# A hybrid trunk on one core: the second mixer's output projection in two parts, and the small triangular blocks ahead of the score blocks

## The chip, the core and the metric

The kernel runs on one core of a Trainium2 chip. The core has five engines with queues of their own, which meet only at semaphores: TensorE (PE in the profile, with its weight loads as PEld) multiplies, VectorE (DVE) and ScalarE (ACT) read and write both the core's memory and the banks into which TensorE writes, GpSimd (POOL) works on the core's memory alone, and SyncE (SP) issues the transfers. The metric is the device time of one execution in microseconds (us).

## What is computed

Two layers on 512 tokens of width 1024, each a mixer and an MLP with residuals, and a last norm. Everything is float32. The change is in layer 1:

```python
h = _rmsnorm(x, norm_mix[1])
p = h @ odd_w_in[0]                              # 1024 -> 2720
o_c = _rwkv7(p[..., :RWKV_IN], ...)              # 8 heads of 64: a recurrence over the tokens
o_d = _conformer_conv(p[..., RWKV_IN:], ...)     # gate, 31 taps in time, LayerNorm, swish: 512 channels
m = concatenate([o_c, o_d])                      # 512 + 512 channels
x = x + m @ odd_w_out[0]                         # 1024 -> 1024
f = square(relu(_rmsnorm(x, norm_ffn[1]) @ w_up[1]))
x = x + f @ w_down[1]
...
# inside _rwkv7, per head:
S = S * w_t + sa * (kk_t * a_t) + v_t * k_t ;  y_t = S r_t
```

## The kernel before

**Layout and precision.** Activations lie channels by tokens: tile k of `x` is 128 channels by 512 tokens. Each large product is made of three matmuls of rounded parts, high by high, low by high and high by low, 128x128 weights against 128x512, all summed in one bank (`cuts`, L994; `tile`, L999). A 128x1024 by 1024x512 product for one output tile is 24 such matmuls. Weights come in chunks of 1 MB, sixteen 128x128 blocks: SP loads chunk n into slot n % 2 once `lo_done` frees it, ScalarE rounds it to `w_hi` (`cut_hi`, or `cut` in four pieces), GpSimd then subtracts to `w_lo` in four pieces (L580) after `hi_done`, which comes with the last piece of the chunk. TensorE waits for `lo_done` before a chunk's first block. ScalarE may round chunk n only when chunk n-2's products are done (`gemm_done`).

**The second mixer** is ordered by hand: the lists `PE1`, `DVE1` and `ACT1` give each engine's steps one by one, and steps of different sort stand between each other. The steps:

- `slice t k`: three matmuls (channel tile k) of one of 22 tiles of the input projection, 176 in all; `ROWS` orders the tiles. Tiles 14 to 21 are the convolution's, in pairs (gate and value), 0 and 1 the low-rank parts, the rest k, v and r of four head pairs c = 0 to 3.
- For each head pair c: `zw`, `za`, `ks`, `kn`, `dyn` and `bonus` prepare; `scores c 0..3` multiply 128x256 blocks, which VectorE copies under a mask (`SC`, L1981, two copies a step); `scores c 4` makes the eight 8x8 diagonal blocks (L1352), VectorE picks them (L1990) and inverts them in six rounds of three small operations (`solve`, L2000 to L2004), `x_of` spreads the inverse. `tok_tr` transposes. `tx`, `dx`, `dxt` with level 3 to 6 double the inverse's block size four times, TensorE, ScalarE (`txc`) and VectorE (`xc`) by turns. Then the chain over the four token chunks n: `g` (L1452, L1456), ScalarE copies `G`, `u` (L1464), ScalarE copies `U`, `s` (L1472, L1474), VectorE updates the state `Sp` (L2058), `y` (L1488 to L1492), and `g` of the next n needs `Sp`. `post c 0..2` normalize and gate into `ym`.
- `tap c j`: the convolution on VectorE, 31 steps for each of four channel groups, each adding to the one before. After the last: `conv_mean`, `conv_sub`, squares, `conv_var`, `conv_root`, `conv_spread`, `conv_scale`, `conv_silu`.
- `m i` rounds channel tile i of the mixer's output for the output projection; `out t i` is one channel tile's three matmuls of output tile t. `M_TILES` puts tile 3, the last pair's, last.

Before, all eight channel tiles of an output tile are summed in one bank. `out` steps exist for output tiles 0 and 1 only; tiles 2 to 7 follow the mixer (`out_proj`). VectorE adds each finished tile to `x`, squares it, makes the low part of the normed input (`h_rest`) and adds up the squares (`residual`); ScalarE makes the high part (`h_cut`). `first_up` multiplies MLP tiles 0 and 1 channel tile by channel tile as `h_ready` allows, `stat` sums the squares over channels with 16 small matmuls, and `up(0, 1)` takes the MLP's second weight chunk.

## Time and profile before

| what | us |
|---|---|
| median of three timed runs | 1248.44 |
| lowest and highest | 1248.24 and 1249.92 |
| the profiled execution, device time | 1249.62 |
| its span, first to last instruction | 1247.8 |
| TensorE busy in the span | 1208.0 |
| VectorE busy in the span | 640.9 |
| second mixer with its output projection, first matmul to last | 546.6 to 885.4 |

A busy TensorE is not TensorE at its peak. Matmuls overlap, so a busy time says only that there was one in flight; what a matmul costs in a stream is the distance between two starts. The granted clock says at which of two levels, 2.4 and 1.2 GHz, TensorE ran: 1.00 is the upper.

### The profile page before, as it was taken

What the parts mean: (1) busy time and instruction counts of PE and PEld (TensorE: products, weight loads), DVE (VectorE), ACT (ScalarE), POOL (GpSimd) and SP (SyncE); (2) the same over time, 40 slices, a digit from 0 to 9 for tenths busy, and PEclk for the clock granted to TensorE, in tenths of its full rate; (3) what the DMA queues carried; (4) which work ended last, traced back from release to release, by engine and by line L of the source; (5) the groups of instructions that cost most, each with busy time, mean ns of one, the idle gap of its engine ahead of it and who ended that gap; (6) DMA issues with size and microseconds to landing.
All of it is one profiled execution on the core that took longest, in us unless ns stands there. A gap on an engine that the chain in (4) does not pass through costs nothing. (4 is left out here: it accounts for less than half of the span.)

```text
span 1247.8 us, 19837 instructions
## 1 busy us (share of the span) xinstructions
PE 1208.0 (97%) x7876; PEld 968.2 (78%) x7876; DVE 640.9 (51%) x1032; ACT 399.5 (32%) x578; POOL 501.3 (40%) x368
## 2 busy tenths in 40 slices
PE   7999999999999999999999998989999999999996
PEld 6877778888888888887777766757888888888885
DVE  4524655442114544446789889876545211444333
ACT  5634423222112222226353634343322211222110
POOL 0541435554445555545121220113545444555441
PEclk9999999999999999999999999879999999999998
DMA  7211222222322222231111110102222222222211
GB/s 278 102 68 68 74 96 68 101 101 102 101 101 82 89 98 101 101 101 68 35 69 35 36 68 2 35 2 74 96 102 101 101 101 83 86 101 101 101 67 68
DMA packets 17776, 104.97 MB, mean 84 GB/s; under 512 B 1968, under 2 KB 2480, under 8 KB 6064
## 3 DMA queue, kind: packets, MB, share of 16 engines
q1 hardware_dynamic: 17280, 103.67, 23.9%
q8 instruction: 49, 0.80, 0.3%
q10 hardware_dynamic: 432, 0.38, 0.1%
q14 instruction: 15, 0.12, 0.0%
HBM read 101.94 MB, written 2.10 MB: 83 GB/s over the span
## 5 line engine op out<-in xcount | busy, mean ns | idle before, releaser
L580 POOL TENSOR_TENSOR w_lo<-w_raw,w_hi 128x512 fp32r<-128x512 f32 x360 | 495.6, 1406 | 714.4 <-ACT w_hi L673 266.6
L1013 PE MATMUL ps<-h_hi,w_hi 128*128 128x512 f32 x688 | 275.9, 401 | 0.1
L1013 PE MATMUL ps<-h_lo,w_hi 128*128 128x512 f32 x688 | 268.4, 390 | 0.0
L1013 PE MATMUL ps<-h_hi,w_lo 128*128 128x512 f32 x688 | 268.3, 390 | 0.0
L673 ACT ACTIVATE w_hi<-w_raw 128x2048 fp32r<-128x2048 f32 x50 | 95.7, 1913 | 194.7 <-PE ps L1013 143.4
L1013 PEld LDWEIGHTS ps<-h_hi,w_hi 128*128 128x128 f32 x688 | 129.3, 188 | 35.5 <-issue 8.7
L1013 PEld LDWEIGHTS ps<-h_hi,w_lo 128*128 128x128 f32 x688 | 129.4, 188 | 27.6
L1013 PEld LDWEIGHTS ps<-h_lo,w_hi 128*128 128x128 f32 x688 | 129.5, 188 | 25.7 <-issue 1.0
L1013 PE MATMUL ps<-f_hi,w_hi 128*128 128x512 f32 x384 | 149.4, 389 | 0.0
L1013 PE MATMUL ps<-f_lo,w_hi 128*128 128x512 f32 x384 | 149.4, 389 | 0.0
L1013 PE MATMUL ps<-f_hi,w_lo 128*128 128x512 f32 x384 | 149.4, 389 | 0.0
L1630 DVE TENSOR_TENSOR f_hi<-relu 128x512 f32 x64 | 56.8, 888 | 154.7 <-ACT relu L648 152.8
L648 ACT ACTIVATE relu<-ps 128x512 f32<-128x512 f32 x56 | 33.5, 599 | 223.4 <-PE ps L1013 223.4
L2085 DVE SCALAR_TENSOR_TENSOR cv<-zpad,cols,cv 128x512 f32<-128x512 f32 x120 | 96.5, 804 | 2.3
L1648 DVE TENSOR_TENSOR scaled<-ps,rn 128x512 f32<-128x512 f32 x16 | 11.1, 692 | 146.7 <-PE ps L1013 112.1
L1013 PEld LDWEIGHTS ps<-f_hi,w_lo 128*128 128x128 f32 x384 | 72.1, 188 | 15.0
L1013 PEld LDWEIGHTS ps<-f_hi,w_hi 128*128 128x128 f32 x384 | 72.1, 188 | 15.0
L1013 PEld LDWEIGHTS ps<-f_lo,w_hi 128*128 128x128 f32 x384 | 72.1, 188 | 14.9
L1634 DVE TENSOR_TENSOR f_sq<-relu 128x512 f32<-128x512 f32 x64 | 72.1, 1127 | 0.0
L1658 DVE TENSOR_TENSOR scaled<-ps,rn 128x512 f32<-128x512 f32 x16 | 11.1, 692 | 102.1 <-PE ps L1013 74.9
L598 ACT ACTIVATE w_hi<-w_raw 128x2048 fp32r<-128x2048 f32 x20 | 38.2, 1910 | 58.6 <-PE ps L1013 41.8
L1637 DVE TENSOR_TENSOR f_lo<-f_sq,f_hi 128x512 f32 x64 | 46.0, 718 | 12.3 <-DVE f_sq L1634 12.3
(328 smaller groups left out, 1699.8 us busy)
## 6 DMA issues: line engine op xcount, KB each, us to landing
w_raw<-in_weights SPq DMA_DIRECT2D x91, 1024.0 KB, 4.8
x<-in_xT SPq DMA_DIRECT2D x8, 256.0 KB, 6.5
w_raw<-in_weights SPq DMA_DIRECT2D x8, 256.0 KB, 6.9
outT<-x SPq DMA_DIRECT2D x8, 256.0 KB, 2.0
...
```

What stands on the lines that cost most here:

```text
L580: piece = pool.tensor_tensor(w_lo[:, j, at], w_raw[:, j, at], w_hi[:, j, at].bitcast(f32), SUB)
L598: act.activation(w_hi[:, n % 2, :], w_raw[:, n % 2, :], ACT.Copy).then_inc(s("hi_done"), 1)
L648: act.activation(relu[:, g % 2, :], bank(g % 2), ACT.Relu).then_inc(s("relu_done"), 1)
L673: act.activation(w_hi[:, n % 2, :], w_raw[:, n % 2, :], ACT.Copy).then_inc(s("hi_done"), 1)
L1013: mm = pe.matmul(bank(gb(g) if isinstance(i, int) else g % 2), w, r, start=(k == 0 and m == 0), stop=(k == K - 1 and m == 2))
L1630: tt(f_hi[:, bass.ds(4 * i + c, 1), :].rearrange("p a n -> p (a n)"), relu[:, g % 2, :], relu[:, g % 2, :], MUL).then_inc(s("fhi_done"), 1)
L1634: tt(f_sq[:, :], relu[:, g % 2, :], relu[:, g % 2, :], MUL).then_inc(s("fsq_done"), 1)
L1637: tt(f_lo[:, bass.ds(4 * i + c, 1), :].rearrange("p a n -> p (a n)"), f_sq[:, :], F(f_hi[:, bass.ds(4 * i + c, 1), :].rearrange("p a n -> ...
L1648: tt(scaled[:, j, :], bank((gd + j) % 2), rn[:, :], MUL)\
L1658: tt(scaled[:, d % 2, :], bank(g % 2), rn[:, :], MUL).then_inc(s(f"gemm_evac{g % 2}"), 1)
L2085: stt(cv[:, c, :], zpad[:, c % 2, j:j + SEQ], col("conv_w", TAPS * c + j), cv[:, c, :], MUL, ADD)\
```

## The change

The output projection's channel tiles are split into seven early ones (pairs 0 to 2 and the convolution) and the late one of the last pair, tile 3. The early parts of all eight output tiles are `out` steps in `PE1`, most of them between the steps of the last pair's chain; VectorE adds them to `x` (`add t`). The late part is 24 matmuls after the mixer (`late`), with a second addition to `x` (`late_adds`). The squares for the norm move to ScalarE (`late_cuts`) and their channel sums to TensorE, 16 small matmuls for each channel tile between the parts of `first_up` (`late_sums`). The weights' chunks are packed in the new order, with 3, 2, 2 and 1 finished tiles to the four chunks. `scores c 4` becomes `corner c` and goes ahead of the four `scores` steps, into banks 4 and 6. The taps of two channel groups have semaphores of their own and take turns. The convolution's projection tiles come earlier in `ROWS`, and all three lists are new. Semaphores of the set-up are merged.

```diff
+EARLY_M, LAST_M = [0, 1, 2, 4, 5, 6, 7], 3
+KE = len(EARLY_M)
+OUT1 = [3, 2, 2, 1]
-ROWS = [0, 2, 4, 3, 14, 15, 5, 7, 6, 1, 16, 17, 8, 10, 9, 18, 19, 11, 13, 12, 20, 21]
+ROWS = [0, 2, 14, 15, 4, 3, 5, 7, 16, 17, 6, 1, 8, 10, 18, 19, 9, 20, 21, 11, 13, 12]
...
+        def tap_done(c, n):
+
+            return s(f"tap_done{c % 2}"), TAPS * (c // 2) + n
...
+            ("out", 6, 0), ("out", 6, 1), ("y", 3, 3), ("out", 6, 2), ("out", 6, 3), ("post", 3, 0),
...
+            def late_cuts():
+
+                for k in range(KD):
+                    h_cut(3, k)
+                    if k >= 2:
+                        act.wait_ge(s("late_sums"), k - 1)
+                    act.activation((xsq, ssq)[k % 2][:, :], x[:, k, :], ACT.Square).then_inc(s("late_sq"), 1)
+                    for part in {5: (0,), 6: (1, 2), 7: (3,)}.get(k, ()):
+                        if part == 0:
+                            act.wait_ge(s("late_mm"), KD)
+                        cut(N_MLP1 + 1, part)
+                load_sqrt(3)
...
+            def late(t):
+
+                at = KE * KD + t
+                n, blk = N_OUT1 + at // 16, at % 16
+                if t == 0:
+                    pe.wait_ge(s("lo_done"), n + 1)
+                    pe.wait_ge(s("m_lo_done"), 2 * KD)
+                if t == 3:
+                    for last in (6, 7):
+                        pe.wait_ge(*evacuated(FIRST_TILE[N_OUT1] + last))
+                if t >= 5:
+                    pe.wait_ge(s("late_add"), t - 4)
+                for m, (w, r) in enumerate(cuts(n % 2, blk, LAST_M, M_HI1[LAST_M], M_LO1[LAST_M])):
+                    mm = pe.matmul(bank(late_bank(t)), w, r, start=(m == 0), stop=(m == 2))
+                mm.then_inc(s("late_mm"), 1)
+
+            def late_sums(k):
+
+                pe.wait_ge(s("late_sq"), k + 1)
+                for t in range(TT):
+                    for q in range(0, P, 32):
+                        mm = pe.matmul(ps[q:q + 32, 7, t:t + 1], (xsq, ssq)[k % 2][:, t * P + q:t * P + q + 32], ONES[:, 0:1],
+                                       start=(k == 0 and t == 0), stop=(k == KD - 1 and t == TT - 1))
+                mm.then_inc(s("late_sums" if k < KD - 1 else "stat_done"), 1)
...
-                        pe.wait_ge(s("lo_done"), nu + 1)
+                        if layer == 0:
+                            pe.wait_ge(s("lo_done"), nu + 1)
+                        else:
+                            late(0)
+                            late(1)
                         for k in range(KD):
+                            if layer and k + 2 < KD:
+                                late(k + 2)
+                            if layer and k == 0:
+                                pe.wait_ge(s("lo_done"), nu + 1)
                             pe.wait_ge(*wait_k(k))
...
+                            if layer:
+                                late_sums(k)
...
-            out_proj(N_OUT1 + 1, N_MLP1, M_HI1, M_LO1)
             mlp(1)
...
+            def late_adds():
+
+                for t in range(KD):
+                    dve.wait_ge(s("late_mm"), t + 1)
+                    tt(x[:, t, :], x[:, t, :], bank(late_bank(t)), ADD).then_inc(s("late_add"), 1)
+                    h_rest(3, t)
...
+            def add(t):
+
+                g = FIRST_TILE[N_OUT1] + t
+                dve.wait_ge(s("gemm_done"), g + 1)
+                tt(x[:, t, :], x[:, t, :], bank(g % 2), ADD).then_inc(s(f"gemm_evac{g % 2}"), 1)
...
-            residual(N_OUT1, 3)
+            late_adds()
             mlp(1)
```

What TensorE has in a row at three places. First, in the last pair's chain, from its second `g` (state and scores) over `u`, `s` and `y` to its third, before:

```order
L1452 MATMUL ps<-Sp,AR 64x64 x4
L1456 MATMUL ps<-vtok,SC 64x64 x4
L1490 MATMUL ps<-SC,U 64x128 x2
L1492 MATMUL ps<-SC,vtok 64x128 x2
L1464 MATMUL ps<-G,XT 64x64 x4
L1472 MATMUL ps<-U,btok 64x64 x2
L1474 MATMUL ps<-vtok,ktok 64x64 x2
L1488 MATMUL ps<-AR,Sp 64x128 x2
L1490 MATMUL ps<-SC,U 64x128 x2
L1492 MATMUL ps<-SC,vtok 64x128 x2
L1452 MATMUL ps<-Sp,AR 64x64 x4
```

and now, from the same `g` up to its `u` and a part of what follows:

```order
L1526 MATMUL ps<-Sp,AR 64x64 x4
L1530 MATMUL ps<-vtok,SC 64x64 x4
L1629 MATMUL ps<-m_hi,w_hi 128x512
L1629 MATMUL ps<-m_lo,w_hi 128x512
L1629 MATMUL ps<-m_hi,w_lo 128x512
L1629 MATMUL ps<-m_hi,w_hi 128x512
L1629 MATMUL ps<-m_lo,w_hi 128x512
L1629 MATMUL ps<-m_hi,w_lo 128x512
L1538 MATMUL ps<-G,XT 64x64 x4
L1629 MATMUL ps<-m_hi,w_hi 128x512
```

The parts of the output projection have moved in between the chain's steps.

Second, around the last `y` (L1488 to L1492) of the third pair's chain, with the last pair's first `scores` ahead of it, before:

```order
L1340 MATMUL ps<-AR,kT 128x256 x2
L1488 MATMUL ps<-AR,Sp 64x128 x2
L1490 MATMUL ps<-SC,U 64x128 x2
L1492 MATMUL ps<-SC,vtok 64x128 x2
L1013 MATMUL ps<-h_hi,w_hi 128x512
L1013 MATMUL ps<-h_lo,w_hi 128x512
L1013 MATMUL ps<-h_hi,w_lo 128x512
L1013 MATMUL ps<-h_hi,w_hi 128x512
L1013 MATMUL ps<-h_lo,w_hi 128x512
L1013 MATMUL ps<-h_hi,w_lo 128x512
L1340 MATMUL ps<-AR,bT 128x256 x2
```

and now (L1414 is `corner`, L1427 `scores`, L1449 and L1451 `tok_tr`):

```order
L1414 MATMUL ps<-AR,bT 32x32 x32
L1538 MATMUL ps<-G,XT 64x64 x4
L1562 MATMUL ps<-AR,Sp 64x128 x2
L1564 MATMUL ps<-SC,U 64x128 x2
L1566 MATMUL ps<-SC,vtok 64x128 x2
L1427 MATMUL ps<-AR,bT 128x256 x2
L1427 MATMUL ps<-AR,kT 128x256 x2
L1427 MATMUL ps<-AR,bT 128x256 x2
L1427 MATMUL ps<-AR,kT 128x256 x2
L1427 MATMUL ps<-AR,bT 128x256 x2
L1427 MATMUL ps<-AR,kT 128x256 x2
L1449 MATMUL ps<-cen,vT 128x128 x4
```

The projection's slices that stood here have moved ahead of the third pair's chain.

Third, in the MLP's first two tiles, where before the 48 matmuls stood in one row, now for each channel tile:

```order
L1108 MATMUL ps<-m_hi,w_hi 128x512
L1108 MATMUL ps<-m_lo,w_hi 128x512
L1108 MATMUL ps<-m_hi,w_lo 128x512
L1151 MATMUL ps<-h_hi,w_hi 128x512
L1151 MATMUL ps<-h_lo,w_hi 128x512
L1151 MATMUL ps<-h_hi,w_lo 128x512
L1151 MATMUL ps<-h_hi,w_hi 128x512
L1151 MATMUL ps<-h_lo,w_hi 128x512
L1151 MATMUL ps<-h_hi,w_lo 128x512
L1116 MATMUL ps<-mats,ssq 32x1 x16
```

The late part (L1108) and the sums of squares (L1116) have moved in between.

## Rows read from the trace of the kernel before

**Rows 1.** Busy time by stretch; columns as in its first row (PEclk: granted clock).
```profile
core 0: us, PE busy (x) PEld busy (x) DVE busy (x) ACT busy (x) POOL busy (x), PEclk, DMA share, GB/s
766.25:797.75 31.50, 27.04 (x338) 18.32 (x337) 26.01 (x66) 12.35 (x25) 5.44 (x4) 1.00 0.10 35
797.75:818.10 20.35, 18.78 (x282) 14.62 (x282) 19.02 (x33) 5.22 (x14) 0.00 (x0) 0.75 0.01 2
804.00:814.00 10.00, 9.96 (x139) 8.39 (x136) 9.45 (x17) 0.93 (x3) 0.00 (x0) 0.50 0.01 2
821.00:831.30 10.30, 8.99 (x91) 6.28 (x86) 8.30 (x14) 2.14 (x6) 0.00 (x0) 0.50 0.00 0
546.60:886.30 339.70, 320.50 (x3420) 239.33 (x3418) 271.35 (x522) 146.99 (x300) 82.52 (x60) 0.96 0.14 48
```

**Rows 2.** TensorE in order of time: start, us, line, idle before.
```profile
766.25 0.45 PE L1456 MATMUL ps<-vtok,SC 128*64 128x64 f32 x8
797.75 1.12 PE L1398 MATMUL ps<-xc,SC 64*64 64x32 f32 x32
818.10 0.45 PE L1456 MATMUL ps<-vtok,SC 128*64 128x64 f32 x8 [0.41 <-ACT XT L913]
885.36 0.39 PE L1076 MATMUL ps<-h_hi,w_hi 128*128 128x512 f32 x1
896.18 0.39 PE L1076 MATMUL ps<-h_lo,w_hi 128*128 128x512 f32 x1
896.41 0.39 PE L1076 MATMUL ps<-h_hi,w_lo 128*128 128x512 f32 x1
896.73 0.43 PE L1037 MATMUL ps<-mats,ssq 128*32 128x1 f32 x32
897.09 0.50 PE L1013 MATMUL ps<-h_hi,w_hi 128*128 128x512 f32 x1
```

**Rows 3.** TensorE's waits from 560 to 900 us: total, times, longest.
```profile
PE ps L1452 <- DVE Sp L2058: 4.1, 8, 0.6
PE ps L1340 <- DVE SC L1981: 3.5, 4, 1.4
PE ps L1464 <- ACT G L926: 3.4, 9, 0.4
```

**Rows 4.** VectorE in order of time: a lone tap, last pair's scores and inversion, chained taps.
```profile
757.52 0.70 DVE L2085 SCALAR_TENSOR_TENSOR cv<-zpad,cols,cv 128x512 f32<-128x512 f32 x1
758.13 0.29 DVE L2023 COPY_PREDICATED xc<-masks,ps 128x128 f32<-128x128 uint8 x1
...
788.74 1.35 DVE L1981 COPY_PREDICATED SC<-masks,ps 128x512 f32<-128x512 uint8 x2
789.99 1.00 DVE L1990 COPY_PREDICATED lt<-masks,ps 128x64 f32<-128x64 uint8 x4
791.82 0.22 DVE L2000 STREAM_SHUFFLE r<-z 128x64 f32<-128x64 f32 x1
792.60 0.22 DVE L2000 STREAM_SHUFFLE r<-z 128x64 f32<-128x64 f32 x1
796.99 0.71 DVE L2016 STREAM_TRANSPOSE xc<-xtc 128x512 f32<-128x512 f32 x1
814.83 5.47 DVE L2085 SCALAR_TENSOR_TENSOR cv<-zpad,cols,cv 128x512 f32<-128x512 f32 x7
```

**Rows 5.** VectorE, ScalarE and GpSimd at the residual, and one rounding piece (L812).
```profile
885.56 0.69 DVE L1612 TENSOR_TENSOR x<-x,ps 128x512 f32<-128x512 f32 x1 [0.90 <-PE ps L1013]
887.04 0.75 DVE L1593 SCALAR_TENSOR_TENSOR h_lo<-x,cols,h_hi 128x512 fp32r<-128x512 f32 x1
886.29 0.72 ACT L624 ACTIVATE h_hi<-x,cols 128x512 fp32r<-128x512 f32 x1 [4.71 <-DVE x L1612]
836.28 0.62 ACT L812 ACTIVATE w_hi<-w_raw 128x512 fp32r<-128x512 f32 x1
888.89 5.03 POOL L580 TENSOR_TENSOR w_lo<-w_raw,w_hi 128x512 fp32r<-128x512 f32 x4 [5.39 <-ACT w_hi L598]
```

More of the change, by code:

```diff
@@ L428, in build @@
-            ("scores", 3, 4), ("slice", 21, 2), ("conv_mean", 0), *run("tok_tr", 3, 0, 3), ("post", 2, 0),
-            *run("slice", 21, 3, 8), ("tx", 3, 3, 0), ("tx", 3, 3, 1), ("post", 2, 1), ("dx", 3, 3, 0),
[5 rows of a table removed]
-            ("u", 3, 3), ("y", 3, 3), *run("conv_var", 0, 4), ("out", 0, 2), ("conv_spread",), ("post", 3, 0),
-            ("post", 3, 1), *run("out", 1, 0, 3), ("post", 3, 2), ("out", 0, 3), ("out", 1, 3), ("out", 0, 4),
-            ("out", 1, 4), ("out", 0, 5), ("out", 1, 5), ("out", 0, 6), ("out", 1, 6), ("out", 0, 7), ("out", 1, 7),
+            ("slice", 0, 3), ("slice", 2, 3), ("stat",), ("slice", 0, 4), ("slice", 2, 4), ("slice", 0, 5),
@@ new lines, in build @@
+            ("dx", 2, 4, 1), ("slice", 12, 0), ("slice", 12, 1), ("post", 1, 2), ("slice", 12, 2), ("slice", 12, 3),
[4 rows of a table added]
+            ("g", 2, 3), ("corner", 3), ("u", 2, 3), ("y", 2, 3), *run("scores", 3, 0, 3), ("tok_tr", 3, 0),
+            ("scores", 3, 3), ("tok_tr", 3, 1), ("tok_tr", 3, 2), ("post", 2, 0), ("conv_mean", 0),
+            ("conv_mean", 1), ("tx", 3, 3, 0), ("tx", 3, 3, 1), ("dx", 3, 3, 0), ("dx", 3, 3, 1), ("conv_mean", 2),
+            ("conv_mean", 3), ("tx", 3, 4, 0), ("tx", 3, 4, 1), ("dx", 3, 4, 0), ("dx", 3, 4, 1), ("post", 2, 1),
@@ L438, in build @@
+            *run("out", 7, 2, 7),
         ]
         DVE1 = [
[L441 to L444 removed]
@@ new lines, in build @@
+            ("zero", 4), ("evac_a", 2), ("zero", 5), ("zero", 6), ("evac_b", 2), ("evac_a", 14), ("evac_b", 14),
+            ("evac_a", 15), ("ks_v", 0), ("scan", 0), ("kn_v", 0), ("dyn", 0, "at"), ("evac_a", 4),
+            ("dyn", 0, "ab"), *run("tap", 0, 0, 4), ("evac_a", 3), ("dyn", 0, "bt"), ("evac_b", 4), ("evac_b", 3),
+            ("dyn", 0, "k2"), ("dyn", 0, "kt"), ("dyn", 0, "rt"), ("dyn", 0, "rk"), ("evac_a", 5), ("bonus", 0),
+            ("tap", 0, 4), ("corner", 0), ("solve", 0, 6), ("evac_b", 5), ("solve", 0, 5), ("solve", 0, 4),
@@ new lines, in build @@
+            ("solve", 0, 3), ("scores", 0, 0), ("dec", 0), ("evac_a", 7), ("scores", 0, 1), ("tap", 0, 5),
+            ("scores", 0, 2), ("evac_a", 16), *run("tap", 0, 6, 9), ("solve", 0, 2), ("scores", 0, 3),
+            ("tap", 0, 9), ("evac_b", 7), ("evac_b", 16), ("scan", 1), ("solve", 0, 1), ("x_of", 0), ("evac_a", 17),
+            ("tap", 1, 0), ("tap", 0, 10), ("tap", 1, 1), ("tap", 1, 2), ("tap", 0, 11), *run("tap", 1, 3, 9),
+            ("dx", 0, 3, 0), ("ks_v", 1), ("tap", 1, 9), ("tap", 0, 12), ("evac_a", 6), ("dx", 0, 3, 1),
@@ new lines, in build @@
+            ("evac_b", 18), ("tap", 1, 25), ("evac_a", 19), ("dxt", 1, 5), ("tap", 2, 0), ("tap", 2, 1),
+            ("post_v", 0, 2), ("tap", 2, 2), ("dyn", 2, "rk"), *run("tap", 2, 3, 7), ("tap", 1, 26), ("tap", 2, 7),
+            ("evac_a", 9), ("post_v", 0, 3), ("s", 1, 0), ("evac_b", 9), ("bonus", 2), ("tap", 1, 27),
+            ("corner", 2), ("s", 1, 1), ("tap", 2, 8), ("tap", 1, 28), ("tap", 2, 9), ("solve", 2, 6),
+            ("tap", 2, 10), ("tap", 1, 29), *run("tap", 2, 11, 14), ("tap", 1, 30), ("tap", 2, 14), ("s", 1, 2),
@@ new lines, in build @@
+            ("tap", 2, 15), ("tap", 2, 16), ("evac_a", 20), ("solve", 2, 5), ("solve", 2, 4), ("solve", 2, 3),
+            ("solve", 2, 2), ("tap", 2, 17), ("solve", 2, 1), ("evac_b", 20), ("scores", 2, 0), ("evac_a", 21),
+            ("tap", 3, 0), ("scores", 2, 1), ("tap", 3, 1), ("evac_a", 11), ("scores", 2, 2), ("evac_b", 11),
+            ("tap", 3, 2), ("x_of", 2), ("tap", 3, 3), ("scores", 2, 3), ("tap", 3, 4), ("tap", 2, 18),
+            *run("tap", 3, 5, 8), ("scan", 3), ("tap", 3, 8), ("post_v", 1, 0), ("tap", 3, 9), ("tap", 3, 10),
@@ L2149, in rest @@
         return r
-    out += rest(i["even_w_out"][0], i["w_up"][0], i["w_down"][0])
+    out += rest([_both(i["even_w_out"][0], R(256 * n), R(256 * n + 128)) for n in range(4)], i["w_up"][0], i["w_down"][0])
     xw, xg = list(range(1536, 1600)), list(range(1600, 1696))
```

361 lines of the change are left out of this document (178 added, 183 removed), and 38 rows, old and new, of tables (ACT1, PE1).

## The prediction

> **What bounds the kernel now.** I looked first at busy time by stretch, then at TensorE's order of time, then at who waits for whom, then at VectorE's order, always inside the second mixer, since the change leaves the rest as it is. The row for the whole mixer and projection [rows 1] gives TensorE 320.5 of 339.7 us busy and VectorE 271.4. So TensorE is the bound on average, with 19.2 us of true idle, and VectorE, at 80%, has little room. The idle time is in handoffs of a chain: above all the state update and the copy of `G` [rows 3], 0.4 to 0.6 us each. Beside it, two stretches of 10 us have a granted clock of 0.50, the lower of the two levels (1.2 GHz), right where the last pair's inversion and chain leave TensorE's matmuls small and scattered [rows 1]. They cost up to 5 us each. That and the last chain's waits is what the change can win at the end; the question is what it gives for it.
>
> I cut the time from the first matmul of the mixer (546.6) to the first of the MLP's second weight chunk (897.09) into five stages at marks that both versions have [rows 2]: third pair's chain begins (766.25), last pair's first `tx` (797.75), last pair's chain begins (818.10), `first_up` begins (885.36), `up(0, 1)` begins (897.09).
>
> **Unit costs.** A matmul of 128x512 takes 0.23 us from start to start (896.18 to 896.41) [rows 2], so a slice or an `out` part takes 0.69. A switch to a small group costs 0.09 more (0.32 from 896.41 to 896.73), and I take 0.2 for going and coming back. Sixteen sums take 0.36. On VectorE a lone tap takes 0.61 until the next instruction starts (757.52 to 758.13); in a row where each waits for the one before, seven take 5.47, so 0.79 [rows 4]. A `scores` pair is 1.25, the diagonal pick 1.0, a `solve` round 0.78, `x_of` 1.5 [rows 4].
>
> **Stage 1, to the third pair's chain.** The lists, counted, put 176 slices here instead of 165: 11 x 0.69 = 7.6 us of TensorE work that comes earlier and is not new. Other work up to the mark is equal. Against it stand waits that the new order can avoid: most of the 3.5 us for `SC` [rows 3], since other steps now stand between the score blocks. But the first pair's chain loses half of its cover of slices, which at 0.4 to 0.55 a handoff gives back some 1.4. VectorE has 4 fewer us of chained taps in the whole mixer (28 chained ones against 66 in the lists, 0.12 each), and enough lead here: by counts it reaches each handoff some 18 to 25 us of own work earlier than TensorE does, and starts some 19 later. So TensorE still sets the pace. 7.6 - 3.0 = 4.6: **+4.6**.
>
> One rule of the Trainium skill speaks about the taps. VectorE: DVE Perf Modes, section The DRAIN you can't avoid, has it that a next instruction waits for the pipe to empty, chained or not. Then alternating two groups would save nothing. By that rule the sum would be up to 4 us longer where VectorE is the bound; the trace has 0.61 alone and 0.79 in a chain, so it disagrees, and the measurement is used.
>
> **Stage 2, to the last pair's first `tx`.** Before: 31.5 us with TensorE 27.0 busy and VectorE 26.0 [rows 1]. The 11 slices are gone from here, so TensorE has about 27.0 - 7.6 + 2.1 (two sums of the convolution) = 21.5. VectorE has more: 12 taps instead of 8, six steps of `dyn`, three copies out, the state updates, four score pairs (5.0), the pick (1.0), six rounds (4.7), `x_of` (1.5); with 12 x 0.68 for the taps, between the lone and the chained one, I get 28.7. `tx` needs the inverse, so VectorE decides. Its head waits for `g`, `u`, `s` (2.5), and 1 us for score blocks. **32 us, +0.5**, and TensorE stands still for 8 to 10 of them. The corner blocks that lead don't shorten this: VectorE is full from end to end.
>
> **Stage 3, to the last chain.** Before 20.35, 10 of it at the low clock. Without the one `out` part and its wait that is 19.3; at full clock maybe 15.5. Now `conv_var`, `conv_spread` and three parts replace two `conv_mean`: +3.2, and VectorE has the convolution's end and the last taps between the turns: I come to 19.5 for the turns. Then 13 more `out` parts stand ahead of `g`: 9.0. The clock: this stretch and the one before are as scattered as the ones that fell to 0.50 before, so I add 3; for VectorE beside a weight chunk on GpSimd I allow 1.5, which no row prices alone. **33.0 us, +12.7**, of which 16 parts (11.0) are work brought forward.
>
> **Stage 4, to the end of the early projection.** Before 67.26. Now 40 parts x 0.69 = 27.6, the chain's own matmuls and `post` 10.8, 14 switches x 0.2 = 2.8: **41.2 us, -26.1**. No wait is left: between a `g` and its `u` stand two parts, 1.4 us, against 0.4 for the copy; `Sp` is covered by one or two. The weight chunks come in time: a chunk needs four roundings (0.62 each, 0.5 start to start) and GpSimd's 5.0 [rows 5], about 8 to 10 with what ScalarE does between, while TensorE has 11 to 12 us before it needs the block. That cover is thin: 2 us.
>
> **Stage 5, to `up(0, 1)`.** Before 11.73. Now 24 late matmuls (5.5), 48 (10.9), eight sums (8 x 0.36 = 2.9) and some 16 half switches (1.8): 21.1. Waits on top: the first `h_ready` needs the addition (0.69), the high part (0.72), the low part (0.75) [rows 5], 2.3 us after `late(0)`, with 1.4 of cover: 0.9. The last such one adds 0.4. Then the new one: the chunk for `up(0, 1)` may be rounded only after all eight late tiles (`late_mm`), and its pieces stand between two `h_cut`s and two squares. From the end of `late(7)`: 4 pieces (2.1), two `h_cut`s (1.4), two squares (1.1), about 4.7; GpSimd 5.0 and latencies: done at 10. TensorE has for that only the last three channel tiles, 3 x (1.4 + 0.36 + 0.2) = 6. It stands 4 us. 21.1 + 0.9 + 0.4 + 3.8 = **26.2 us, +14.5**. Before, its lower part was done at 888.89 + 5.03 = 893.9 [rows 5], 3 us ahead of the 897.09 of `up(0, 1)`.
>
> **Sum.** 4.6 + 0.5 + 12.7 - 26.1 + 14.5 = +6.2. The profiled execution took 1249.62, so 1255.8; the median of the runs is 1.2 lower: **1254.6 us**.
>
> **Bounds of what no row shows.** The clock in stages 2 and 3: from none low (-3) to 20 us of it on the path (+7). Stage 1: from all waits gone and no loss (-2.5) to VectorE late at the third pair (+4). The chunk wait: 0, if the roundings slip in earlier, to 5. Stage 2: 29.7 (VectorE's work with 1 us of waits) to 35.
>
> **The rivals.** *Faster, the cover works.* VectorE is not the bound in stage 2: it arrives with its taps and scores done, because it worked through the waits of stage 1. Then stage 2 is TensorE's 21.5 and handoffs, 25; with no gap the clock stays at the upper level, 3 less in stage 3. 1254.6 - 7 - 3 = 1244.6, and 1241 with the early waits gone too. For it: VectorE has 68 us free in the mixer [rows 1]. Against: its instructions in stage 2 depend on that stage's own blocks, apart from 12 taps; only without six of them and with `solve` unbroken does it come under 27. It decides if VectorE's busy share in stage 2 is under 85%.
>
> *Nothing moves.* The gain of stage 4 and its price cancel, with the clock term at 0 and half of the chunk wait: 1254.6 - 3 - 2 = 1249.6.
>
> *Slower by more, the clock.* The low level comes with thin activity: before, it came twice around the last pair. Now TensorE has 21.5 of 32 us to do there and then a chain of turns. If some 20 us run at 0.50 with the turns on the path, that is +7 to 1262. The Trainium skill says it too, in TensorE: Matmul & The Clock Gate, What's actually happening: activity releases the throttle and its lack brings it back. By that the emptied stage 2 would lower the clock; the dense rows of stage 4, which replace the second low stretch, speak for the upper level there.
>
> **How the numbers follow.** About 0.2%, 2.5 us, is what a measurement can tell from no change. The forecast (1251 to 1258) 0.50, the clock rival (1258 to 1266) 0.14, nothing moves (1246 to 1251) 0.16, faster 0.20. So slower 0.64, same 0.16, faster 0.20. For 8 in 10 the range goes from 1242 to 1264.
>
> **What would show it.** Right: VectorE over 90% busy between the third pair's chain and the last pair's `tx`, with TensorE's longest waits there on `xc`; no wait of `u` and `s` in the last chain; a wait on `w_lo` of some 4 us at the MLP's second chunk. Wrong: a granted clock of 1.00 throughout and stage 2 under 28 us, or no wait on `w_lo`; then it is faster.

## The result, and the profile after

| | us |
|---|---|
| changed kernel, median of 14 runs | 1257.02 (1253.67 to 1261.63) |
| kernel before, 14 runs beside them | 1249.94 (1244.78 to 1253.86) |
| ratio, with its 95% interval | 1.0067 (1.0052 to 1.0082) |
| profiled execution of the changed kernel, device time and span | 1259.28 and 1256.3 |

The change costs 0.67%, 8.4 us. It was forecast at +6.2, 1254.6 us. The stages have the same marks as in the prediction. First the busy times of the changed kernel by stretch; the columns are those of [rows 1]. The rows are the five stages, then all of them, then what stands behind them.

```profile
547.73:772.93 225.20, 220.24 (x2299) 163.81 (x2297) 188.45 (x381) 106.86 (x223) 54.55 (x40) 0.99 0.15 51
772.93:805.94 33.01, 24.83 (x307) 15.96 (x306) 27.30 (x69) 8.36 (x19) 0.00 (x0) 0.79 0.01 1
805.94:833.91 27.97, 27.82 (x464) 21.71 (x463) 18.36 (x35) 18.90 (x36) 10.14 (x8) 1.00 0.12 40
833.91:874.78 40.87, 40.83 (x327) 29.36 (x327) 9.08 (x16) 11.85 (x25) 14.94 (x13) 1.00 0.23 78
874.78:901.98 27.20, 21.53 (x329) 15.57 (x329) 15.68 (x23) 15.13 (x24) 6.92 (x6) 0.97 0.12 40
547.73:901.98 354.25, 335.25 (x3722) 246.41 (x3720) 258.87 (x520) 161.09 (x327) 86.55 (x65) 0.97 0.14 48
901.98:1256.30 354.32, 344.06 (x1568) 284.56 (x1568) 126.58 (x151) 72.62 (x61) 165.33 (x120) 0.98 0.27 92
```

The kernel before has for the same stretches as a whole, up to its mark 897.09 and from there on:

```profile
546.61:897.09 350.48, 331.27 (x3497) 248.05 (x3495) 273.38 (x524) 151.84 (x305) 87.55 (x64) 0.97 0.15 50
897.09:1247.80 350.71, 340.46 (x1578) 281.85 (x1568) 129.48 (x155) 74.80 (x63) 165.48 (x120) 0.99 0.26 91
```

| stage | before | after | difference | forecast |
|---|---|---|---|---|
| 1, to the third pair's chain | 219.64 | 225.20 | +5.6 | +4.6 |
| 2, to the last pair's first `tx` | 31.50 | 33.01 | +1.5 | +0.5 |
| 3, to the last pair's chain | 20.35 | 27.97 | +7.6 | +12.7 |
| 4, to the end of the early projection | 67.26 | 40.87 | -26.4 | -26.1 |
| 5, to `up(0, 1)` | 11.73 | 27.20 | +15.5 | +14.5 |
| sum of the five | 350.48 | 354.25 | +3.8 | +6.2 |
| behind `up(0, 1)`'s start | 350.71 | 354.32 | +3.6 | 0 |
| ahead of the mixer | 546.61 | 547.73 | +1.1 | 0 |

So the mixer is only 3.8 us longer, and nearly as much again is lost behind it. The 1.1 us ahead of the mixer have no part in the change: over the kernels profiled here that start lies between 545.9 and 548.4.

TensorE's true idle in the five stages is 354.25 - 335.25 = 19.0 us, against 19.2 before. The parts hid the last chain's waits, and others opened. The longest of TensorE's waits in stage 2, and then those in stage 5, of the changed kernel (line that waited, what ended the wait, total us, times, longest):

```profile
PE ps L1427 <- DVE SC L2063: 3.8, 3, 2.1
PE ps L1538 <- ACT G L968: 1.5, 3, 0.8
```

```profile
PE ps L1055 <- POOL w_lo L609: 4.2, 1, 4.2
PE ps L1151 <- issue: 1.0, 1, 1.0
PE ps L1151 <- DVE h_lo L1668: 0.5, 2, 0.4
```

The lower clock moved likewise. These are the stretches of 8 us of the changed kernel in which the granted clock was under 0.99, up to 912 us:

```profile
688.00:696.00 8.00, 7.34 (x132) 6.21 (x131) 5.48 (x12) 3.72 (x8) 5.41 (x4) 0.98 0.10 16
696.00:704.00 8.00, 8.00 (x64) 6.40 (x62) 6.66 (x13) 0.82 (x2) 0.00 (x0) 0.81 0.30 119
...
776.00:784.00 8.00, 5.49 (x68) 3.76 (x66) 6.92 (x13) 2.83 (x7) 0.00 (x0) 0.60 0.00 0
784.00:792.00 8.00, 7.55 (x122) 4.33 (x122) 5.23 (x16) 1.07 (x3) 0.00 (x0) 0.76 0.01 4
792.00:800.00 8.00, 4.19 (x26) 2.99 (x24) 7.67 (x24) 0.17 (x1) 0.00 (x0) 0.88 0.00 0
800.00:808.00 8.00, 7.34 (x116) 5.12 (x116) 7.79 (x18) 4.15 (x9) 0.00 (x0) 0.91 0.01 2
...
896.00:904.00 8.00, 3.85 (x43) 2.83 (x43) 5.74 (x6) 3.08 (x4) 7.93 (x6) 0.78 0.12 16
904.00:912.00 8.00, 8.00 (x30) 6.41 (x29) 4.32 (x5) 0.60 (x1) 4.68 (x3) 0.79 0.53 195
```

With two levels, a mean of 0.81 over 8 us is (1 - 0.81) x 2 x 8 = 3.0 us at the lower one. Added up, the eight rows hold 23.8 us. The same sum for the kernel before, over 720 to 736 and 800 to 832, gives 23.8 too. They lie elsewhere: 13.6 in the third pair's chain and the score blocks behind it, where the slices had been taken out, and 6.8 at the wait for the chunk, from 900.5 to 907.3. The second and third stretch of before, around the last pair, are gone. Neither sum holds the end of the kernel, where the last 11.1 us of the changed kernel are at the lower level and the last 7.0 of the kernel before.

The wait and what follows it, TensorE in order of time (start, us, line, and in brackets the idle time ahead and what ended it):

```profile
901.98 0.80 PE L1055 MATMUL ps<-h_hi,w_hi 128*128 128x512 f32 x1 [4.15 <-POOL w_lo L609]
902.57 0.63 PE L1055 MATMUL ps<-h_lo,w_hi 128*128 128x512 f32 x1
903.00 0.63 PE L1055 MATMUL ps<-h_hi,w_lo 128*128 128x512 f32 x1
```

TensorE stands still for 4.15 us, and then a matmul takes 0.43 from start to start, where it takes 0.23 at the upper level [rows 2]. The clock had come down inside the wait, where it costs nothing; 5.3 of the 6.8 us lie behind the wait, and they cost 2.5: from `up(0, 1)` to the MLP's last large matmul the changed kernel needs 340.4 us and the kernel before 337.9. The other 1.1 of the +3.6 behind the mark lie in the last norm, most of it in eight matmuls that run at the upper level in the kernel before (first row) and at the lower one in the changed kernel:

```profile
1238.87 1.16 PE L1057 MATMUL ps<-mats,rrms 128*128 128x128 f32 x8 [0.60 <-DVE rrms L1578]
1246.43 2.08 PE L1124 MATMUL ps<-mats,rrms 128*128 128x128 f32 x8 [0.59 <-DVE rrms L1653]
```

This end varies from one execution to the next: the lower level has the last 7 to 8 us in seven of the thirteen executions profiled here and the last 10 to 11 in five, with and without a wait for the chunk ahead of it (e11 and the changed kernel; e9 and e1).

### The profile page after: what moved, and what is told of

The parts are those of the page before. It is cut to its first block, busy times and chain, and to the rows that moved or that the text cites. A ratio compares the mean times of both kernels' runs of the same rounds, so it can differ in the third digit from the quotient of the medians.

```text
span 1256.3 us, 20279 instructions
## 1 busy us (share of the span) xinstructions
PE 1216.0 (97%) x8100; PEld 969.6 (77%) x8100; DVE 623.5 (50%) x1023; ACT 406.6 (32%) x599; POOL 500.2 (40%) x368
## 4 chain that ended last, share of the span: by engine, by line
PE 91%; DVE 3%; ACT 2%; POOL 2%; issue 2%; DMA 0%; DVEq 0%; SPq 0%; POOLq 0%; ACTq 0%
PE ps L1055 60%; PE ps L1185 7%; PE ps L1242 4%; PE ps L1629 3%; PE ps L1219 2%; POOL w_lo L609 2%; PE ps L1151 1%; PE ps L1427 1%; PE ps L1472 1%; PE ps L1495 1%; PE ps L1354 1%; PE ps L1108 1%; PE ps L1538 1%; PE ps L1530 0%; PE ps L1124 0%
## 5 line engine op out<-in xcount | busy, mean ns | idle before, releaser
L702 ACT ACTIVATE w_hi<-w_raw 128x2048 fp32r<-128x2048 f32 x50 | 95.6, 1913 | 194.7 <-PE ps L1055 143.4
L1055 PEld LDWEIGHTS ps<-h_hi,w_lo 128*128 128x128 f32 x688 | 130.2, 189 | 27.9
L1055 PE MATMUL ps<-f_hi,w_hi 128*128 128x512 f32 x384 | 149.4, 389 | 0.0
L2167 DVE SCALAR_TENSOR_TENSOR cv<-zpad,cols,cv 128x512 f32<-128x512 f32 x120 | 90.7, 776 | 1.0
L1730 DVE TENSOR_TENSOR scaled<-ps,rn 128x512 f32<-128x512 f32 x16 | 11.1, 692 | 146.7 <-PE ps L1055 112.1
L1740 DVE TENSOR_TENSOR scaled<-ps,rn 128x512 f32<-128x512 f32 x16 | 11.1, 692 | 102.1 <-PE ps L1055 74.9
L1185 PE MATMUL ps<-f_hi,w_hi 128*128 128x512 f32 x128 | 49.8, 389 | 0.0
```

Of the source, the lines that this page charges most:

```text
L702: act.activation(w_hi[:, n % 2, :], w_raw[:, n % 2, :], ACT.Copy).then_inc(s("hi_done"), 1)
L1055: mm = pe.matmul(bank(gb(g) if isinstance(i, int) else g % 2), w, r, start=(k == 0 and m == 0), stop=(k == K - 1 and m == 2))
L1185: mm = pe.matmul(bank((gd + j) % 2), w, r, start=(k == 0 and m_ == 0), stop=(k == HALF_K - 1 and m_ == 2))
L2167: stt(cv[:, c, :], zpad[:, c % 2, j:j + SEQ], col("conv_w", TAPS * c + j), cv[:, c, :], MUL, ADD)\
```

## Experiments

Times are medians, ratios go against runs of the kernel before on the same chip. The stages are those of one execution each, and how much of it ran at the lower level differs between executions of the same steps: the 1.6 us by which e1 and e6 are shorter in stage 1 are such a stretch, at 696. e9's profiled execution is the fastest of its twelve runs. The stages of all profiled executions, in us; the first two rows are those above:

| kernel | 1 | 2 | 3 | 4 | 5 | behind | median | ratio (95%) |
|---|---|---|---|---|---|---|---|---|
| before | 219.6 | 31.5 | 20.4 | 67.3 | 11.7 | 350.7 | 1249.9 | |
| changed | 225.2 | 33.0 | 28.0 | 40.9 | 27.2 | 354.3 | 1257.0 | 1.0067 (1.0052 to 1.0082) |
| e1, roundings earlier | 223.6 | 33.0 | 27.8 | 40.9 | 23.0 | 351.8 | 1249.9 | 1.0005 (0.9989 to 1.0021) |
| e2, wait filled | 225.2 | 33.2 | 27.8 | 40.9 | 27.3 | 350.9 | 1252.6 | 1.0028 (1.0013 to 1.0042) |
| e3, stage 2 filled | 225.1 | 29.7 | 35.9 | 40.9 | 27.2 | 352.3 | 1258.6 | 1.0065 (1.0045 to 1.0084) |
| e4, six taps cut | 225.2 | 31.5 | 35.1 | 40.9 | 27.2 | 352.3 | 1256.8 | 1.0061 (1.0036 to 1.0086) |
| e5, chain bare | 225.2 | 33.0 | 21.9 | 59.2 | 27.8 | 352.2 | 1269.1 | 1.0150 (1.0121 to 1.0178) |
| e6, sums on VectorE | 223.6 | 32.1 | 27.9 | 40.9 | 25.5 | 351.7 | 1252.2 | 1.0011 (0.9994 to 1.0028) |
| e7, corner last | 228.3 | 42.3 | 27.8 | 40.9 | 27.2 | 352.1 | 1267.5 | 1.0139 (1.0109 to 1.0169) |
| e8, e1 and more filled | 225.1 | 29.7 | 30.9 | 40.9 | 23.0 | 351.6 | 1250.4 | 1.0002 (0.9986 to 1.0019) |
| e9, sums in the wait | 225.2 | 29.8 | 27.8 | 40.9 | 22.8 | 350.7 | 1249.6 | 1.0006 (0.9986 to 1.0027) |
| e10, e9 and a little filled | 225.2 | 29.7 | 29.1 | 40.9 | 22.8 | 354.3 | 1249.5 | 1.0009 (0.9987 to 1.0030) |
| e11, e9 with a later low part | 227.5 | 32.8 | 27.8 | 40.9 | 24.6 | 352.9 | 1254.6 (one run; the kernel before beside it 1255.0) | |

### e1: the four roundings earlier

```diff
-                    for part in {5: (0,), 6: (1, 2), 7: (3,)}.get(k, ()):
-                        if part == 0:
-                            act.wait_ge(s("late_mm"), KD)
+                    for part in {1: (0,), 2: (1,), 5: (2,), 6: (3,)}.get(k, ()):
+                        if part >= 2:
+                            act.wait_ge(s("late_mm"), 4 * (part - 1))
```

> The four roundings of the chunk for up(0, 1) stand at channel tiles 1, 2, 5 and 6 instead of 5, 6, 6 and 7; the first two overwrite blocks of output tile 7's early part, the third waits for four late tiles, the fourth for all eight. Theory: the changed kernel loses 4.15 us to the wait for this chunk and, because TensorE stood still, runs some 6 us at the lower clock behind it (0.43 instead of 0.23 from start to start, about 3 us). With the last piece some 3.5 us sooner, GpSimd's 5 us end at about 898.3, so of the wait under 1 us is left and the clock stays up: 1257.0 - 3.7 - 3 = 1250 us, ratio to before 1.001. Rival: the wait only moves to the next chunk or to the sums and the low clock has another cause: under 2 us gained, 1255 or more.

Measured: 1249.9 us. The wait is 0.6, and no lower clock stands behind it. The four pieces of the low part start at 889.90. That is 17.5 us after the stage's start, and in the changed kernel it was 21.3 (896.07), so they come 3.8 us earlier in the stage.

```profile
889.90 5.46 POOL L609 TENSOR_TENSOR w_lo<-w_raw,w_hi 128x512 fp32r<-128x512 f32 x4 [16.45 <-ACT w_hi L854]
895.42 0.50 PE L1055 MATMUL ps<-h_hi,w_hi 128*128 128x512 f32 x1 [0.61 <-POOL w_lo L609]
```

Stage 5 loses 4.2 us and what lies behind it 2.5, together 6.7; the medians are 7.1 apart. (Stage 1 is 1.6 shorter because this execution lacked the stretch at the lower clock at 696.) So where the four roundings stand and what they wait for is worth nearly the whole loss. In the changed kernel ScalarE stood for 2.9 us, waiting for the eighth late tile ahead of its first piece, which needs none of them, and then had all four pieces, two high parts and two squares to do before GpSimd could start; in e1 only the last piece is left behind that tile. The edit changed place and threshold at once, and no run parts the two.

### e2: the wait filled

```diff
                     def up(i, j, wait_k=None):
+                        if layer and half == 0 and isinstance(i, int):
+                            pe.wait_ge(s("late_add"), KD)
+                            for _ in range(16):
+                                pe.matmul(bank(2), H_HI[0][:, 0:P], H_HI[0], start=True, stop=True)
                         pe.wait_ge(s("lo_done"), 2 * i + (nu + j + 1))
```

> 16 added matmuls of 128x512 into a bank that nobody needs stand ahead of the wait for the chunk of up(0, 1); the results are unused. Their 3.7 us lie inside the wait of 4.15. Theory: the low clock behind the wait is due to TensorE standing still, so it stays at the upper level and about 3 us come back with the wait's end unchanged: 1254 us, ratio 1.004. Rival: the low clock comes from elsewhere, or the added work delays the chunk: 1257 us, ratio 1.0067.

Measured: 1252.6. Stage 5 is as long as in the changed kernel, the chunk comes no sooner, and yet 3.4 us come back behind it, 2.5 of them right behind the wait and 0.9 in the kernel's last norm, which the edit doesn't touch:

```profile
896.56 3.92 PE L1162 MATMUL ps<-h_hi 128*128 128x512 f32 x16
900.87 0.50 PE L1055 MATMUL ps<-h_hi,w_hi 128*128 128x512 f32 x1 [0.39 <-POOL w_lo L609]
901.21 0.40 PE L1055 MATMUL ps<-h_lo,w_hi 128*128 128x512 f32 x1
901.45 0.39 PE L1055 MATMUL ps<-h_hi,w_lo 128*128 128x512 f32 x1
```

The starts are 0.23 apart at once, against 0.43 above. A wait of 4.15 us on this path cost 4.2 + 2.5 in the changed kernel's profile, and the second part is the clock alone. It isn't always as much: e3, e4, e5 and e7 have the same wait of 4.15 to 4.18 with 3.4 us at the lower level where the changed kernel has 6.8, and there it costs 1.5. The Trainium skill says in TensorE: Matmul & The Clock Gate, section What's actually happening, that activity releases the throttle and its lack brings it back; the pair of runs agrees.

### e3 and e8: large matmuls in the waits of stages 2 and 3

In e3, with evacuated banks and no use of the results (`warm n` is n matmuls of 128x512):

```diff
+            ("warm", 2), ("u", 2, 1), ("warm", 1), ("s", 2, 1), ("y", 2, 1), ("warm", 2), ("g", 2, 2), ("warm", 1),
+            ("u", 2, 2), ("warm", 1), ("s", 2, 2), ("y", 2, 2), ("bonus", 3), ("g", 2, 3), ("corner", 3), ("u", 2, 3),
+            ("warm", 1), ("y", 2, 3), ("scores", 3, 0), ("warm", 6), ("scores", 3, 1), ("warm", 8), ("scores", 3, 2),
```

> 25 added matmuls of 128x512 with unused results stand in TensorE's waits between the third pair's second u and the last pair's third score blocks, one or two at a handoff, six and eight between score blocks. Theory: stage 2 (33.0 us) loses about 2 to 3 us to the lower clock in the third pair's chain, where slices no longer fill the gaps; with the gaps filled the clock is 1.00 there and the stage takes about 31, total 1254.5. It doesn't get shorter than 29.5, since VectorE has 27.3 us of work in it. Rival A: VectorE sets the whole stage and the clock there costs nothing: 33.0, total 1257. Rival B: the added matmuls delay the handoffs more than the clock gives back: 34, total 1258.

Measured: 1258.6. Stage 2 did what the theory says, 29.7 at a clock of 1.00. But stage 3 grew by 8, which neither side had:

```profile
771.77:801.46 29.69, 26.23 (x330) 16.66 (x329) 27.34 (x69) 8.35 (x19) 0.00 (x0) 1.00 0.01 2
801.46:812.50 11.04, 10.24 (x295) 7.72 (x294) 9.03 (x17) 6.66 (x15) 5.00 (x4) 1.00 0.01 3
812.50:830.00 17.50, 17.43 (x145) 14.36 (x142) 8.77 (x17) 12.34 (x22) 1.21 (x2) 0.51 0.18 62
```

For 17 us, from the end of the convolution's sums (matmuls of one column) and a turn of the inversion on, TensorE is busy nearly without a gap, at half speed. e8 has e1's edit, the same fills, and three more matmuls at each of four places among those turns:

```diff
-("dx", 3, 4, 1), ("post", 2, 1), *run("conv_var", 0, 3), ("post", 2, 2), ("conv_var", 3), ("tx", 3, 5, 0), ("conv_spread",),
+("dx", 3, 4, 1), ("warm", 3), ("post", 2, 1), ("warm", 3), *run("conv_var", 0, 3), ("post", 2, 2), ("warm", 3), ("conv_var", 3),
+("tx", 3, 5, 0), ("conv_spread",), ("warm", 3),
```

> The earlier roundings and the matmuls in the last waits of the third chain, and 12 more of 128x512 (unused results) between the turns of the last pair's inversion, where filling the third chain's waits alone was followed by 17 us at the lower clock from the convolution's small sums on and stage 3 grew from 28.0 to 35.9. Theory: the clock falls behind stretches in which TensorE has only small matmuls; large ones between them keep it up: stage 2 is 29.7, stage 3 about 28 + 2.8, total 1249.9 - 3.3 + 2.8 = 1249.4. Rival: the lower clock comes sooner or later whatever stands there, one stretch of 10 to 17 us around the last pair; then it falls within stages 3 or 4 again and the total is 1255 or more.

```profile
772.44:802.13 29.69, 26.22 (x330) 16.65 (x329) 27.34 (x69) 8.35 (x19) 0.00 (x0) 1.00 0.01 2
802.13:833.01 30.88, 30.74 (x476) 23.59 (x475) 18.89 (x35) 18.90 (x36) 10.18 (x8) 1.00 0.10 36
```

Measured: 1250.4, as the theory has it. 12 matmuls (2.8 us) took away a stretch that had cost 8. That isn't the profiled execution alone: the mean clock is 0.992 to 0.996 in all twelve runs of e8, 0.989 to 0.993 in the twelve of e1, and 0.987 to 0.990 in the six of e3, which also has the wait for the chunk. But 29.69 + 30.88 is 60.6, and e1 without any of it has 60.8: what the clock gives back, the added work takes. So in these runs the clock follows what TensorE does, and unused work buys nothing. Why the changed kernel and e1 run stage 3 at 1.00, with the same steps there as e3, no run settles. It can fall there without added matmuls too: in e4 below it did, for 17 us of this stage.

### e4: six taps cut

```diff
+            SHORT = {(2, 26), (3, 25), (2, 27), (3, 26), (3, 27), (2, 28)}
...
+                    w = 8 if (c, j) in SHORT else SEQ
```

Six of the convolution's taps work on 8 of the 512 columns, so this kernel leaves out a part of the convolution.

> Work is left out: six of the convolution's taps that stand ahead of the last pair's inverse on VectorE handle 8 columns instead of 512, so the convolution's part of the output isn't the reference's. Theory: VectorE sets the end of stage 2, so 6 x about 0.5 us come off it: 33.0 becomes 30.0, total 1254. Rival: the handoffs of score blocks and the clock set it; the taps lie in waits and stage 2 stays at 32.5 to 33, total 1257.

Measured: 1256.8, between the two: stage 2 falls by 1.5, half of the 3.0, and all of it behind the third pair's last state update, which comes 12.95 us into the stage in both kernels. VectorE, which in the changed kernel had no wait from the pick of the corner blocks to the inverse, now waits for score blocks, 0.65 and 0.31 us at two of the four (the idle time stands in brackets):

```profile
792.87 1.33 DVE L2063 COPY_PREDICATED SC<-masks,ps 128x512 f32<-128x512 uint8 x2 [0.65 <-PE ps L1427]
```

So VectorE is the bound of the second half of stage 2, but the score blocks' round trips lie only a microsecond or so behind it. The profiled execution, at 1262.3 the slowest of its five, also had 17 us at the lower clock in stage 3, as e3 had.

### e5: the chain bare

The order of the last pair's chain and of the parts, each line a list of steps (the additions to `x` and the roundings, in VectorE's and ScalarE's lists, move along and aren't shown):

```diff
+            ("g", 3, 0), ("u", 3, 0), ("s", 3, 0), ("y", 3, 0), ("g", 3, 1), ("u", 3, 1), ("s", 3, 1), ("y", 3, 1),
+            ("g", 3, 2), ("u", 3, 2), ("s", 3, 2), ("y", 3, 2), ("g", 3, 3), ("u", 3, 3), ("y", 3, 3), *run("out", 0, 3, 7),
+            ("post", 3, 0), *run("out", 1, 0, 7), ("post", 3, 1), *run("out", 2, 0, 7), ("post", 3, 2), *run("out", 3, 0, 7),
...
```

> Undoes the cover: the last pair's chain runs bare, and all early parts from the fourth of output tile 0 on stand behind its last y, with the additions to x and the roundings of their weights moved behind the chain too. Theory: the parts inside the chain save its handoffs; bare, the chain has about 12 waits of 0.4 to 0.6 us (6 us) and runs at the lower clock for a part (3 us), and gives back 12 switches (2.4): last chain plus projection 7 us longer than 28.0 + 40.9, total 1264. Rival: the parts cost the chain as much as they hide, since the chain's own steps are few: within 2 us, 1257. In both cases stage 5 stays at 27.

Measured: 1269.1, 12 us slower than the changed kernel (10 by the ratios to the kernel before). Stages 3 and 4 together take 81.1 instead of 68.8. The bare chain, by stretch and by TensorE's two longest waits in it:

```profile
826.60:850.00 23.40, 18.81 (x189) 13.27 (x192) 1.36 (x5) 5.55 (x13) 4.94 (x4) 0.56 0.14 46
```

```profile
PE ps L1525 <- ACT XT L950: 3.5, 1, 3.5
PE ps L1533 <- ACT G L963: 2.0, 4, 0.8
```

With those for `U` and `Sp` the waits are 8 us, of which the 3.5 for the finished inverse (`XT`) had not been in the expectation, and a clock of 0.56 over 23.4 us is 20.6 us at the lower level. In the changed kernel TensorE was busy for 40.83 of 40.87 us there, at 1.00. Of the 12.2 us, the waits make 8, so that some 4 are left for the clock, an estimate, since the switches that fall away and the moved roundings weren't measured by themselves. The cover works, and that is part of its worth.

### e6, e9 and e11: who adds up the squares

e6 takes e1 and has VectorE add ScalarE's squares, with one sum over channels at the end:

```diff
+                        if t > 1:
+                            dve.wait_ge(s("late_sums"), t - 1)
+                        tt(ssq[:, :], ssq[:, :], (xsq[:, :], scaled[:, 0, :])[t % 2], ADD).then_inc(s("late_sums"), 1)
...
-                            if layer:
-                                late_sums(k)
```

> On top of the earlier roundings (1249.9): VectorE adds up the squares that ScalarE makes, and TensorE sums them once, with 16 small matmuls instead of 8 x 16 amid first_up. Theory: TensorE's seven sums less (0.36 each) and seven switches less (0.15 each) come off a stretch in which TensorE is the bound: stage 5 from 23.0 to 19.4, if the chunk's low part is there in time; it comes with the eighth late tile, which is 6 x 0.5 = 3 us sooner as well, so most is kept: 1246.9, ratio 0.998. VectorE has 2.1 us a channel tile against TensorE's 2.1. Rival: the addition delays the low part h_lo and TensorE waits for it: 1250, ratio 1.0005.

Measured: 1252.2, and stage 5 is 25.5, longer than e1's 23.0. The rival held: TensorE waits 4.6 us for `h_lo`, six times, because the addition stood behind the low part. e9 puts it into the 0.79 that VectorE waits for ScalarE:

```diff
                     tt(x[:, t, :], x[:, t, :], bank(late_bank(t)), ADD).then_inc(s("late_add"), 1)
+                    if t > 1:
+                        late_square(t - 1)
                     h_rest(3, t)
```

> The same as with the sums of squares on VectorE, but each addition stands between x's addition and the low part, where VectorE waits 0.79 us for ScalarE's high part, and not behind the low part. Theory: behind the low part it made a period of 2.74 us a channel tile (0.68 + 0.79 + 0.75 + 0.68 less overlaps) against TensorE's 2.1 to 2.3, and TensorE waited 4.6 us on h_lo; inside the wait the period is about 2.15, so the waits on h_lo go and stage 5 falls from 25.5 to about 20 to 21, total 1249.9 - 2.5 = 1247.4, ratio 0.998. Rival: ScalarE's high part and square, or the chunk's low part for up(0, 1), set the pace: stage 5 stays at 23, total 1250.

Measured: 1249.6, and stage 5 is 22.8, hardly shorter than e1's 23.0, though TensorE waits for `h_lo` only twice, 0.5 and 2.2 us, at the last two channel tiles. The loss is in the last one. VectorE and GpSimd of e9:

```profile
884.72 0.69 DVE L1698 TENSOR_TENSOR ssq<-ssq,scaled 128x512 f32<-128x512 f32 x1
885.60 0.75 DVE L1669 SCALAR_TENSOR_TENSOR h_lo<-x,cols,h_hi 128x512 fp32r<-128x512 f32 x1 [0.19 <-ACT h_hi L653]
...
886.86 1.66 DVE L1698 TENSOR_TENSOR ssq<-ssq,xsq 128x512 f32<-128x512 f32 x1
888.44 1.74 DVE L1669 SCALAR_TENSOR_TENSOR h_lo<-x,cols,h_hi 128x512 fp32r<-128x512 f32 x1
886.68 6.33 POOL L609 TENSOR_TENSOR w_lo<-w_raw,w_hi 128x512 fp32r<-128x512 f32 x4 [15.39 <-ACT w_hi L855]
```

As soon as GpSimd makes the chunk's low part, the same two operations take 1.66 and 1.74 instead of 0.69 and 0.75. e11 tests that, with the fourth rounding behind the eighth square (`7: (3,)` instead of `6: (3,)`):

> The kernel with the sums in VectorE's wait, its chunk's fourth rounding one channel tile later (behind the eighth square), so that GpSimd starts its low part some 2 us later, behind VectorE's last h_lo. Theory: VectorE's last three operations on the core's own memory took 1.66, 1.74 and 1.77 us, where the ones before took 0.69 and 0.75, because GpSimd worked at the same time; now the sum of the seventh square and the last low part take 0.69 and 0.75 again, TensorE's wait of 2.17 us for h_lo falls under 0.6, and the wait for the chunk's low part grows by 1 to 1.5 instead, with stage 5 at 23 to 24. Rival: those durations belong to the operations or to ScalarE's cuts beside them; they stay at 1.7 and stage 5 grows by the whole 2 us.

```profile
891.86 0.68 DVE L1698 TENSOR_TENSOR ssq<-ssq,xsq 128x512 f32<-128x512 f32 x1
892.74 0.75 DVE L1669 SCALAR_TENSOR_TENSOR h_lo<-x,cols,h_hi 128x512 fp32r<-128x512 f32 x1 [0.19 <-ACT h_hi L653]
893.82 7.67 POOL L609 TENSOR_TENSOR w_lo<-w_raw,w_hi 128x512 fp32r<-128x512 f32 x5 [17.53 <-ACT w_hi L855]
899.87 0.79 PE L1056 MATMUL ps<-h_hi,w_hi 128*128 128x512 f32 x1 [4.30 <-POOL w_lo L609]
```

The durations fall back to 0.68 and 0.75, and TensorE's longest wait for `h_lo` to 0.5. In their place stands a wait of 4.30 for the chunk, where it had been 0.7 and 1 to 1.5 more were expected. Stage 5 is 24.6, longer than the 23 to 24 expected: the durations go the way of the theory, and the stage grows by 1.8, nearly what the rival said. The lower level comes inside the wait and lasts 6.8 us, 4.6 of them behind it, much as in the changed kernel. It is one run of its kernel; the row's durations, not its time, are the evidence.

### e7: the corner blocks last again

For the last pair alone (TensorE's list is shown; VectorE's and the semaphore waits follow it):

```diff
-("g", 2, 3), ("corner", 3), ("u", 2, 3), ("y", 2, 3), *run("scores", 3, 0, 3), ("tok_tr", 3, 0), ("scores", 3, 3), ...
+("g", 2, 3), ("u", 2, 3), ("y", 2, 3), *run("scores", 3, 0, 4), ("corner", 3), ("tok_tr", 3, 0), ...
```

> Undoes one part for the last pair alone: its 8x8 corner blocks come behind its four score blocks again, and VectorE picks and inverts them after its copies of the scores, with the same taps in between. Theory: VectorE is full from the third pair's last state update on (27.3 us of work in 33.0), so the order of its work moves the inverse by no more than its waits, 1 us: stage 2 is 33 to 34, total 1257 to 1258. Rival: the lead of the corner is what hides the scores' round trips; without it VectorE waits for each of the four score blocks and the six rounds stand alone behind them: 36 us, total 1260.

Measured: 1267.5, 9 to 10 us slower than the changed kernel; even the rival was too mild. Stage 2 is 9.2 longer. (The 3 us in stage 1 are lower clock that the edit has no part in.) VectorE's longest waits in that stage:

```profile
DVE SC L2070 <- PE ps L1434: 5.6, 4, 2.0
DVE Sp L2147 <- PE ps L1573: 2.7, 2, 1.7
```

A score block's round trip (TensorE's multiplication, VectorE's copy, then the next) takes 2.6 us at the upper clock, of which VectorE works 1.3 and a tap 0.7; the rounds of the inversion had filled the rest. Now they stand behind the four trips, and TensorE, busy for 29.1 of 42.3 us, runs 20.5 us at the lower clock from 797 on, beside the 10.2 in the third pair's chain. How the 9 us divide between the exposed trips and that clock no run shows.

### e10: e9 with a little filled

The fills of e3, and one matmul where e8 has three.

> The same, with the 25 added matmuls in the third chain's and the scores' waits, and four instead of twelve between the last turns. Theory: a few large matmuls keep the clock up at a third of the price: stage 2 29.7, stage 3 29, total 1247.4 - 3.3 + 1.0 = 1245, ratio 0.996. Rival: four are too few, 10 to 17 us at the lower clock fall in stage 3 as they did with none, stage 3 is 34 to 36 and the total 1252.

Measured: 1249.5, so the 1245 was missed. Stage 3 is 29.1 and both stages are at 1.00, as the theory says. The median of the runs' mean clocks rises to 0.993 from e9's 0.989, so the clock that the added matmuls bring is there in the other runs too; their time is the same as e9's. In the profiled execution 6.8 us at the lower clock come 1.3 us behind the wait of 2.2 us for the last `h_lo`; the profiled execution of e9 had the same wait without them. None of the kernels is faster than the one before; e1, e6, e8, e9 and e10 are level with it, within 0.2 to 0.3%.

## Why the prediction was right, point by point

**The direction and the time** held, the time in part by luck. The ratio puts the changed kernel at +8.4 us, with an interval from 6.5 to 10.2, and the forecast of +6.2 is a little short of it. But stage 3 was put 5.1 us too high, and against it stand 1.0 too little in each of stages 1, 2 and 5 and the 4.7 outside the five stages, which the sum had at nothing. The step that was missing is the end of the sum: it stopped at `up(0, 1)`, and the clock behind the wait cost 2.5 more in the profiled execution; the other 1.1 behind the mark and the 1.1 ahead of the mixer no run ties to the change. The clock term had been put into stages 2 and 3.

**Stage 1** (+4.6, measured +5.6): the counted 11 slices are there. The changed kernel's idle time in it is 5.0 against 7.8, so the avoided waits are 2.8 net, close to the 3.0 of the sum. The prediction's own terms don't give that 3.0: "most of the 3.5", less the 1.4 that it gives back, is at most 2.1, and of the 3.5 only 2.9 lie ahead of the third pair's chain. The 1.6 to e1's 223.6 are the stretch at the lower clock at 696.

**Stage 2** (+0.5, measured +1.5) came out near for a reason only half right. "VectorE decides" holds from 786 on; up to there it waits for the third pair's chain, and its share is 83%, where over 90% was named as the sign. TensorE's longest waits were on `SC`, not on `xc`. That chain runs at the lower clock. Together with 3.4 us of it further on that costs 3.3 (e3), and e9 shows the same without an added matmul: its profiled execution has 3.4 us at the lower level in the stage instead of 13.6, and the stage takes 29.8. The sentence that the leading corner blocks don't shorten the stage was wrong by 9 us, clock included (e7). It counted VectorE's work and left out its dependence on TensorE: with the slices gone, the rounds are the only thing that fills the score blocks' trips.

**Stage 3** (+12.7, measured +7.6): 16 parts, 11.0, are there. What was too much were the 3 us for the clock, which was 1.00, and the 1.5 for VectorE beside GpSimd, since VectorE was busy for 18.4 of 28.0 and the profile has no wait of TensorE in this stage. That the clock can fall there at a price of 8 is what e3 shows, so the missing 3 us are partly the luck of this execution.

**Stage 4** (-26.1, measured -26.4) held in its terms, with a busy share of 99.9%. e5 gives the worth of the cover alone: 12 us over stages 3 and 4.

**Stage 5** (+14.5, measured +15.5): the wait of 3.8 for the chunk was 4.15, and e1 shows that it came from the place and the threshold (`late_mm`) of its roundings, as the prediction has it. TensorE's waits for the first and last `h_ready`, put at 1.3, were 1.5.

**The rivals.** "The cover works" needed VectorE's share under 85%, and 83% it was; yet the stage didn't come near 25 us. With the clock at 1.00 it still takes 29.7 (e3), since VectorE has 27.3 us of work in it; the lower clock in the chain, which had lost its slices, made up the rest. "The clock", at 1262, was right in kind: it fell on stage 2 (13.6 us at the lower level) and at the wait, not on the turns.
